# The order of the expert weights' requests, and a wait for the landing of the tile before last

## The reference

```python
scores = jax.nn.sigmoid((t @ p['w_router']).astype(jnp.float32))
...
_, e_idx = lax.top_k(jnp.where(e_mask, biased, -jnp.inf), TOP_K)
...
gte = jnp.einsum('td,edf->tef', t, p['w_gate_e'])
upe = jnp.einsum('td,edf->tef', t, p['w_up_e'])
routed = jnp.einsum('tef,efd->td', jax.nn.silu(gte) * upe * combine[:, :, None], p['w_down_e'])
shared = (jax.nn.silu(t @ p['w_gate_s']) * (t @ p['w_up_s'])) @ p['w_down_s']
return (routed + shared).reshape(b, s, d)
```

## Time and profile before

| What | Value |
|---|---|
| median of three runs | 937.55 us (936.71 to 939.01) |
| the profiled execution, whole | 939.12 us |
| its span, first to last instruction | 937.0 us |
| TensorE busy | 879.6 us (94%) |
| VectorE, ScalarE, GpSimd busy | 35%, 21%, 16% |
| moved by DMA | 325.46 MB, mean 347 GB/s |
| granted TensorE clock | 0.985, full in the whole expert stage |

### The profile page before, as it was taken

How to read it: one execution, slowest core, us unless ns; L and a number is a source line. 1 busy time by engine, 2 the same in 40 slices (tenths; PEclk the granted TensorE clock), 3 DMA queues, 4 the chain that set the end, 5 groups by cost and what they waited for, 6 DMA issues and landing times.

```text
span 937.0 us, 18106 instructions
## 1 busy us (share of the span) xinstructions
PE 879.6 (94%) x7475; PEld 566.4 (60%) x7475; DVE 327.8 (35%) x794; ACT 199.2 (21%) x507; POOL 154.3 (16%) x185
## 2 busy tenths in 40 slices
PE   4999999998899899999899999999999999989897
PEld 3788888876566568746755555554555554545452
DVE  2325570046344498526323212212122122121214
ACT  2000110316123299024111111111011111111012
POOL 0000000032277000000212122121121221212110
PEclk9999999998899899999999999999999999999999
DMA  9966766736499847999899999999999999999994
GB/s 361 399 225 243 291 245 254 285 114 238 147 328 336 327 187 258 414 418 382 336 420 421 418 422 420 418 417 425 417 423 417 421 421 421 420 421 421 420 398 145
DMA packets 61236, 325.46 MB, mean 347 GB/s; under 512 B 16321, under 2 KB 25394, under 8 KB 40610
## 3 DMA queue, kind: packets, MB, share of 16 engines
q1 hardware_dynamic: 47218, 305.53, 81.0%
q0 software_dynamic: 12176, 18.56, 5.9%
q10 hardware_dynamic: 1760, 0.20, 0.2%
HBM read 326.65 MB, written 15.81 MB: 365 GB/s over the span
## 4 chain that ended last, share of the span: by engine, by line
PE 35%; DMA 12%; SPq 2%; DVE 1%; issue 0%; ACT 0%
PE bank L2382 17%; PE bank L2322 9%; PE bank L2333 4%; DMA slot_b<-in_w_e 4%; DMA x<-in_w_e 4%; DMA row_of<-in_w_e 4%; PE bank L2298 2%; SPq L1658 1%; PE bank L2392 1%; PE bank L2368 1%; SPq L1666 1%; DVE slot_b L2704 0%; DVE slot_b L2712 0%; PE bank L2352 0%; ACT slot_b L2533 0%
## 5 line engine op out<-in xcount | busy, mean ns | idle before, releaser
L420 PE MATMUL bank<-h,ring 128*128 128x264 f32 x608 | 138.4, 388 | 0.5 <-PE bank L420 0.3
L420 PEld LDWEIGHTS bank<-h,ring 128*128 128x128 f32 x608 | 114.6, 190 | 21.9 <-issue 2.8
L2606 DVE TENSOR_TENSOR hh<-sge,bank 64x256 f32<-64x256 f32 x64 | 27.1, 423 | 257.3 <-ACT sge L2515 250.2
L1678 POOL DMA_INDIRECT xg<-tok_rows,tab_g x32 | 32.1, 1002 | 331.6 <-PE bank L2298 321.6
L2515 ACT ACTIVATE sge<-bank 64x256 f32<-64x256 f32 x64 | 24.2, 378 | 271.2 <-PE bank L2382 271.2
L2322 PE MATMUL bank<-ring,ht 128*32 128x512 f32 x320 | 72.5, 595 | 8.7 <-DMA x<-in_w_e 4.5
L2382 PE MATMUL bank<-done_out,xt 128*64 128x256 f32 x704 | 78.4, 381 | 0.8 <-DVE ht L2614 0.8
L2382 PE MATMUL bank<-ring,xt 128*64 128x256 f32 x672 | 77.2, 382 | 0.3 <-ACT xt L2506 0.3
L2562 DVE COPY sq<-bank 128x512 f32<-128x512 f32 x64 | 44.2, 691 | 73.3 <-PE bank L2322 73.3
L2382 PEld LDWEIGHTS bank<-done_out,xt 128*64 128x64 f32 x704 | 50.5, 137 | 30.2 <-issue 7.2
L2382 PEld LDWEIGHTS bank<-ring,xt 128*64 128x64 f32 x672 | 46.8, 137 | 34.9 <-issue 14.1
(11 more groups left out here) (489 smaller groups left out, 1303.3 us busy)
## 6 DMA issues: line engine op xcount, KB each, us to landing
ring<-in_w_units SPq DMA_DIRECT2D x25, 2048.0 KB, 11.4
done_out<-in_w_e SPq DMA_DIRECT2D x22, 2048.0 KB
ring<-in_w_e SPq DMA_DIRECT2D x20, 2048.0 KB
slot_b<-in_w_e SPq DMA_DIRECT2D x11, 2048.0 KB
slot_f<-in_w_e SPq DMA_DIRECT2D x10, 2048.0 KB
ring<-in_w_e SPq DMA_DIRECT2D x19, 1024.0 KB
slot_b<-in_w_e SPq DMA_DIRECT2D x10, 1024.0 KB
done_out<-in_w_e SPq DMA_DIRECT2D x10, 1024.0 KB
```

Of the source, the lines that this page charges most:

```text
L420: mm = pe.matmul(bank[:, t % NB, 0:T], w[:, j, k, :], h[:, k, :], start=(k == 0), stop=(k == KD - 1))
L1678: pool.indirect_dma_start(xg[q % AHEAD][:, :], None, tok_rows, bass.IndirectOffsetOnAxis(ap=tab_g[:, q:q + 1].bitcast(U32), axis=0), bound ...
L2606: dve.tensor_tensor(hh[e % 2][:, :], sg[e % 2][:, :], bank[LB:2 * LB, 4 + e % 2, 0:FE], ALU.mult).then_inc(hh_ready, 1)
```

## The change

`load_gu` gets a second wait: the gate/up of expert n is requested only when that of expert n - 2 has landed, in all its 16 parts. In SP's loop the pair's two down tiles are requested ahead of the gate/up of the same step, where they stood behind it. In the same way, the halves of the last down tiles wait for the landing of gate/up 62 and 63.

```diff
+            def landed_gu(sp, e):
+                sp.wait_ge(gu_in[e % SLOTS], 16 * gu_times(e))
+
             def load_gu(sp, e):
                 if e >= SLOTS:
+                    landed_gu(sp, e - 2)
                     sp.wait_ge(gu_done, e - SLOTS + 1)
...
                         for e in range(NE):
-                            if e + SLOTS < NE:
-                                load_gu(sp, e + SLOTS)
                             if e % 2 and 3 <= e < NE - 7:
                                 for n in (e + 3, e + 4):
                                     if n != EXTRA:
                                         load_dn(sp, n)
+                            if e + SLOTS < NE:
+                                load_gu(sp, e + SLOTS)
                             if e == NE - 6:
+                                landed_gu(sp, NE - 2)
                                 load_dn_halves(sp, NE - 4)
                             if e == NE - 5:
+                                landed_gu(sp, NE - 1)
                                 load_dn_halves(sp, NE - 2)
```

## The result

| | before | changed |
|---|---|---|
| median, 9 runs each | 937.55 us | 941.97 us |
| ratio of the times | | 1.0050, 95% interval 1.0031 to 1.0069 |
| profiled execution, span | 937.0 us | 940.7 us |

The changed kernel is slower by 0.50%, 4.7 us, with an interval of 2.9 to 6.5 us. The ratio comes from all executions and not from the two medians, which differ by 4.4 us. The forecast was 941.5 us.

The account below looks back on a forecast made before the run. The weight stream, 1.8 us a pair slower than TensorE, was taken to bound the kernel through expert 59's down tile and the work behind it. +3.5 + 0 + 0.5 + 0 = +4.0 on 937.55 gave 941.5 us, range 935.5 to 944.5.

Parts of the forecast that it names:

- (a) The order: Last pairs: TensorE waits for gate/up 61 instead of the down tile, one gate/up later; +3.53 us, bounds 0 and 7.06.
- (b) The waits for landings: SP's queue: one gate/up and two down tiles, 10.0 us, remain when it goes on, so it never runs dry; 0.
- (c) The start: Start of the expert stage: shallow queue, holes at gate/up 9 and 11; +0.5 us, bounds 0 and +4.0.
- (d) The engines in step: 16 DMA engines, slowest 5.5 us behind the mean: limiting the lead gives nothing back; 0, bounds -5.5 and 0.
- Engines in step: Rival, no change: the lagging engine takes over what leaders leave, up to 5.5 us back, 937.0 us; chance 0.28, wholly or partly.
- A quicker stream: Rival, faster: a bounded backlog speeds all engines over 440 us of stream; 1% gives 937.1 us, 2% 932.7; chance 0.08.
- Holes in every pair: Rival, slower: slow wake-up behind landings rests engines 0.3 us in each of 27 pairs, +8 us, 949.5; chance 0.05.
- signs: TensorE's waits move to odd gate/ups, 1.7 us each, some two pairs earlier; no SP issue takes 8 us.

Follow-up runs that it names:

- last_only: Kernel before with one pair swapped: gate/up 61 requested behind down tiles 58 and 59, no waits for landings; 939.31 us, ratio 1.0050.
- both_ends_back: Changed kernel with the old request order up to e = 9 and in the last two pairs, waits kept; 936.99 us, ratio 1.0016 to the kernel before.
- wait_alone: Changed kernel with its waits for landings but the loop's requests in the old order; 936.25 us against 936.78 for the kernel before, ratio 0.9994.
- two_pairs_back: Changed kernel with gate/up 59 and 61 requested ahead of their down tiles again; 937.94 us against 935.67 for the kernel before, ratio 1.0021.
- last_back: Changed kernel with only gate/up 61 requested ahead of its down tiles again; 939.68 us, ratio 1.0042 to the kernel before.
- swap_alone: Changed kernel without its three waits for landings, new request order kept; 939.66 us against 936.78 for the kernel before, ratio 1.0041.
- after_filled: Changed kernel with 32 repeated matrix products on TensorE ahead of gate_up(61); 942.84 us against 935.67 for the kernel before, ratio 1.0081.
- last_only_filled: Kernel before with gate/up 61 behind its down tiles, and 32 repeated products on TensorE filling the wait ahead of gate_up(61); ratio 1.0035.

## Why the prediction was right

**(a) The order, +3.5 us.** Right, and shown. Gate/up 61 landed at 903.20 us against a forecast of about 902.9, the down projection of 58 and 59 started 3.75 us later than before, and swapping a single pair costs the whole. That it is paid once, and in the last pairs, is shown by the profiles of last_only and both_ends_back, and the times agree. The reason that nothing else gets late held as well: gate/up 62 started at 913.68 us, forecast 913.45.

**(b) The waits for landings, 0.** Right in the sum: wait_alone is level (-2.1 to +1.0 us). In one point it was wrong: I said that one gate/up and two down tiles always stand in the queue, but ahead of gate/up 63 stands gate/up 62 alone, and the busy share fell to 0.70. The hole lies where TensorE is the bound, so it has no price.

**(c) The start, +0.5 us out of 0 to 4.** By the rate too small: the changed kernel lost 1.05 us there. Other profiles with the swapped start have 392 to 409 GB/s from 480 to 520 us, so 0.95 to 2.6 us; those with the old start 413 to 419. The stages start up to 6 us apart, so a fairer stretch is the one from 20 to 60 us behind each stage's own start: 412 to 419 GB/s with the old start, and with the swapped one 408 (changed), 395 (two_pairs_back), 394 (last_back), 390 (swap_alone) and 389 (after_filled), so 1.05 to 2.9 us. By the landing it is less. The last tile waited for landed 442.0 to 442.6 us behind the stage's start in the five profiles with the old start, and 443.0 (changed), 444.3 (two_pairs_back) and 444.4 us (swap_alone) with the swapped one, so 0.4 to 1.8 us later than before. The mechanism stands, and its size is between a tenth and three quarters of the bound. What may move it is TensorE's clock, since SP waits for TensorE there: among the five with the swapped start only the changed kernel began at full clock. The first gate/up took 5.1 to 5.4 us in place of 3.67 in three of the others, and swap_alone's clock fell at 468 us. No run tests that.

**(d) The engines in step, 0 out of -5.5 to 0.** How far the lag shrank is less clear than one pair of profiles suggests. The reckoning made on the earlier trace rows needs the GB/s of the 21 us behind the last landing. In order: the changed kernel, two_pairs_back and both_ends_back, with waits for landings, then swap_alone, last_only and last_only_filled without.

```profile
903.20:924.20 21.00, 20.95 (x180) 10.51 (x180) 4.46 (x9) 3.69 (x7) 1.94 (x2) 1.00 0.87 321
903.42:924.42 21.00, 20.75 (x172) 9.90 (x176) 5.68 (x13) 3.31 (x6) 2.85 (x3) 1.00 0.85 316
897.82:918.82 21.00, 20.75 (x172) 9.90 (x176) 5.67 (x13) 3.31 (x6) 2.85 (x3) 1.00 0.83 315
901.90:922.90 21.00, 20.96 (x168) 10.96 (x172) 3.78 (x8) 3.66 (x7) 1.94 (x2) 0.92 0.79 305
896.32:917.32 21.00, 20.95 (x156) 11.18 (x160) 3.24 (x7) 2.37 (x6) 1.94 (x2) 0.86 0.77 296
898.66:919.66 21.00, 20.96 (x180) 10.51 (x180) 4.47 (x9) 3.69 (x7) 1.94 (x2) 1.00 0.80 307
```

For the changed kernel that is 6.74 MB, so 1.65 MB or 3.9 us of lag. The others come out at 4.2, 4.2, 4.7, 5.2 and 4.6 us. With the waits it is thus 3.9 to 4.7 us (wait_alone 4.7), without them 4.6 to 5.5: if the waits shrink the lag, it is by a little. In the changed kernel the estimate is also capped, as only gate/up 62 had been requested beyond the awaited tile, 2.1 MB or 5.0 us. No view here tells the 16 engines apart, so which of them lag is not shown. What it gave can't be seen: wait_alone's landing is no sooner than before. The changed kernel's is 0.7 us sooner than its hole of 1.05 us would have it, but swap_alone's, with no waits, is 0.8 us sooner than its own hole would have it. So the 0 stands, and the forecast's +0.5 for (c) and (d) together met +0.4 in the profile's landing; that it came so close is in part luck, as the start alone varied by more than 1 us between profiles.

**The price that was left out.** No term of the sum had the clock. A longer wait at one place can drop it, and then 32 products cost 1.6 to 3 us more. In the changed kernel's profile it fell behind a wait of 2.5 us in an earlier pair, as these two rows show (16 products in 3.48 us, and a clock of 0.61), and not in the last one:

```profile
778.69 3.48 PE L2388 MATMUL bank<-done_out,xt 128*64 128x256 f32 x16 [2.50 <-DMA done_out<-in_w_e]
```

```profile
778.00:780.00 2.00, 1.31 (x6) 0.77 (x8) 0.00 (x0) 0.00 (x0) 0.00 (x0) 0.61 0.97 393
```

The same wait, of 2.4 to 3.0 us, and the same fall stand in last_back, two_pairs_back, both_ends_back and after_filled, and both_ends_back's stage is no longer than before all the same: the later pairs' 1.8 us of slack can take that up. A fall at the last wait is not made good. It may be in the median, which moved by 4.4 us where the profile moved by 3.7, but no run separates that.

**The rivals.** Engines in step: at most a small change in step, and none in the time. A quicker stream: 418 and 420 GB/s, no. Holes in every pair: no. What I named as signs came: the waits moved to odd gate/ups, the first at 746.67 us, two pairs ahead of the kernel before, whose first gap stands at 778.64, and no single issue of SP took longer than 1.44 us, where the kernel before had up to 9.17. Only the size of the waits, 0.45 to 1.5 us with two of 2.5 and 2.7, was below the 1.7 forecast for most.

## What to carry to other kernels

When a stage is bound by a stream of tiles, ask which work is still to be done behind the last tile that is waited for: in this kernel two requests that changed places cost the work of the consumer that stands between them, once, in the last rounds, and not in every round. A loss in the middle is made good at the rate at which the consumer is quicker than the stream (here 1.8 us a pair), so only its last rounds and the holes in the stream count. A tile is complete with its slowest engine, and bounding how far requests run ahead did not bring that one in sooner here. And look for long waits: one behind which TensorE's clock is low costs more than the time waited.

## What the runs showed of the hardware

After some 440 us of stream, the slowest of the 16 DMA engines was, by the estimate above, 4.6 to 5.5 us behind their mean in four kernels, and 3.9 to 4.7 us in four that wait for landings. A wait of TensorE of 2.74 us dropped its granted clock to the lower level in one kernel (0.50 in the stretch from 902 to 904 us, and 5.23 us for products that take 3.67), and one of 2.73 us in another kernel did not. One of 5.72 us dropped it (6.53 us); with 3.6 us of products placed in that wait it stayed at the upper level. The Trainium skill, "TensorE: Matmul & The Clock Gate", section "What's actually happening", calls the engine after an idle time cold, at 1.2 GHz; swap_alone's 0.50 behind its wait agrees with that level.
